# A fused two-model kernel on one core: the feed-forward's first projection with the weight tile as the stationary operand

## The reference

```python
def rms_norm(x, g):
    y = x * rsqrt(mean(x * x, axis=-1) + 1e-6)      # one factor per row, "rs" below
    return y * g
def swiglu(x, w1, w2):                               # w1: 1024 x 5632, w2: 2816 x 1024
    gu = x @ w1
    g, u = gu[..., :2816], gu[..., 2816:]
    return (silu(g) * u) @ w2
x = x + 0.5 * swiglu(rms_norm(x, norm), w1, w2)      # factor 1.0 in place of 0.5 in the last two
```

## Time and profile before

| what | us |
|---|---|
| median of 3 runs (2015.02 to 2015.93) | 2015.71 |
| the profiled execution's own time | 2013.65 |
| its span in the profile | 2011.8 |
| PE busy | 1993.3 (99%) |
| DVE busy | 1222.3 (61%) |
| ACT busy | 1027.0 (51%) |
| POOL busy | 282.6 (14%) |

### The profile page before, as it was taken

One profiled execution on the slowest core, in us unless ns is written; L12 is line 12 of the kernel. 1 busy time (PEld: TensorE's weight loads), 2 busy tenths in 40 slices (PEclk: granted clock), 3 DMA queues, 4 the chain that ended last, 5 costly groups with the idle time before them and its releaser, 6 DMA issues.

```text
span 2011.8 us, 26376 instructions
## 1 busy us (share of the span) xinstructions
PE 1993.3 (99%) x9796; PEld 1647.4 (82%) x9796; DVE 1222.3 (61%) x1438; ACT 1027.0 (51%) x1318; POOL 282.6 (14%) x365
## 2 busy tenths in 40 slices
PE   8999999999999999999999999999999999999998
PEld 7888887788888888887788888888888888788886
DVE  5555799865546555798855556556565555545554
ACT  5444676754444444686654436454554445455443
POOL 1000469200000000468200002111100000000000
PEclk9999999999999999999999999999999999999999
DMA  7554454455554554554445544443435554415552
GB/s 268 200 187 175 173 204 160 176 188 188 188 188 186 184 188 183 181 196 165 178 176 197 186 183 168 148 148 144 147 126 209 188 188 168 176 66 200 187 187 94
DMA packets 54627, 354.16 MB, mean 176 GB/s; under 512 B 7696, under 2 KB 8336, under 8 KB 12816
## 3 DMA queue, kind: packets, MB, share of 16 engines
q1 hardware_dynamic: 53968, 352.51, 48.5%
q10 hardware_dynamic: 576, 0.53, 0.1%
HBM read 351.97 MB, written 1.05 MB: 175 GB/s over the span
## 4 chain that ended last, share of the span: by engine, by line
PE 89%; DVE 6%; ACT 2%; DVEq 1%; issue 1%; DMA 0%; SPq 0%; POOLq 0%; ACTq 0%; POOL 0%
PE psum L1953 63%; PE psum L2010 18%; DVE wlo L1104 3%; PE psum L2088 1%; PE psum L2025 1%; DVE psum L1331 1%; PE psum L2425 1%; PE psum L2446 1%; PE psum L1965 1%; PE psum L2432 1%; ACT whi L587 1%; DVEq L1323 1%; PE psum L2136 0%; DMA raw<-w_stream 0%; PE psum L2165 0%
## 5 line engine op out<-in xcount | busy, mean ns | idle before, releaser
L1104 DVE TENSOR_TENSOR wlo<-raw,whi 128x2048 fp32r<-128x2048 f32 x325 | 751.5, 2315 | 388.8 <-ACT whi L587 386.4
L1953 PE MATMUL psum<-whi,xTh 128*128 128x512 f32 (+1 forms) x1920 | 763.2, 398 | 5.1 <-DVE xTl L1121 3.9
L1953 PE MATMUL psum<-whi,xTl 128*128 128x512 f32 (+1 forms) x1920 | 745.0, 388 | 0.0
L1953 PE MATMUL psum<-wlo,xTh 128*128 128x512 f32 (+1 forms) x1920 | 744.6, 388 | 0.0
L587 ACT ACTIVATE whi<-raw 128x2048 fp32r<-128x2048 f32 x325 | 622.0, 1916 | 238.3 <-PE psum L2010 151.6
L1953 PEld LDWEIGHTS psum<-whi,xTh 128*128 128x128 f32 x1920 | 360.7, 188 | 81.8 <-issue 6.3
L1953 PEld LDWEIGHTS psum<-whi,xTl 128*128 128x128 f32 x1920 | 360.5, 188 | 75.6
L1953 PEld LDWEIGHTS psum<-wlo,xTh 128*128 128x128 f32 x1920 | 361.2, 188 | 68.0
L2010 PE MATMUL psum<-whi,braT 128*128 128x512 f32 x1056 | 337.8, 390 | 0.0
L2010 PEld LDWEIGHTS psum<-whi,braT 128*128 128x128 f32 x1056 | 198.2, 188 | 41.2
L2010 PE MATMUL psum<-wlo,braT 128*128 128x512 f32 x528 | 205.5, 389 | 0.0
(11 more groups left out here) (258 smaller groups left out, 1460.5 us busy)
## 6 DMA issues: line engine op xcount, KB each, us to landing
raw<-w_stream SPq DMA_DIRECT2D x326, 1024.0 KB, 4.8
bias<-chunks SPq DMA_DIRECT2D x18, 256.0 KB, 5.0
x<-x_in SPq DMA_DIRECT2D x2, 512.0 KB, 5.3
raw<-w_stream SPq DMA_DIRECT2D x4, 256.0 KB, 7.6
arena<-gate_w SPq DMA_DIRECT2D x2, 512.0 KB, 5.0
arena<-fins SPq DMA_DIRECT2D x2, 512.0 KB, 5.5
con<-consts SPq DMA_DIRECT2D x1, 720.0 KB, 11.1
out<-x ACTq DMA_DIRECT2D x2, 256.0 KB, 2.3
```

The lines of the kernel that those rows point to most:

```text
L1104: TT(wlo[:, r], raw[:, r], whi[:, r].bitcast(F32), ALU.subtract).then_inc(lo_done, 1)
L1953: ins = pe.matmul(dst(rb), s(kt)[:, rows], w[:, r, at_:at_ + cols], start=start and n == 0 and k == 0, stop=stop and n == len(kts) - 1 and ...
```

## The change

The first projection is turned round. A 128x128 tile of the weights is stationary and x moves; what comes out has the columns of h on the partitions, so h needs no transposes (`turn_h` is gone). `xTh` and `xTl` become two halves of one tensor `xT`, and one move of 512 columns takes both parts of x past `whi`. The third product, `wlo` against the high part of x, is a move of 256 columns. For each of the 8 contraction tiles and 4 groups of 128 weight columns there is one wide (512) and one narrow (256) move: 32 wide and 32 narrow in a unit, where 48 wide ones stood. Moves of one width are put in groups of 4 or 8. The high-times-high and high-times-low sums lie in two halves of a bank, and must be added. `up` uses four banks: 0 to 3 in unit 0, 4 to 7 in all others.

After it, ACT copies the low half of the gate out of PSUM (`copied`), DVE adds the high half and multiplies by rs, ACT takes silu, ACT and DVE copy and add the up half, DVE multiplies, ACT makes h's high part and DVE its low part, all on tiles of 128 x 512. As rs now runs along the free dimension, it is needed as a row on every partition: ACT's DMA queue stores rs to memory (`rs_dram`) and loads it back broadcast into `rs_row`, once in each feed-forward. The up half is left without rs, and the residual multiplies by `rs_out` (rs times 0.5 or 1.0, a new POOL instruction ahead of `r_done`).

The diff, cut to its core:

```diff
-        xTh, xTl = sb("xTh", [P, KT, S], F32R), sb("xTl", [P, KT, S], F32R)
+        xT = sb("xT", [P, KT, 2, S], F32R)
+        xTh, xTl = xT[:, :, 0], xT[:, :, 1]
...
+        def up_bank(j):
+            return 0 if isinstance(j, int) and j == 0 else 4
...   ACT, ffn
                 split(b, 0)
+                act.wait_ge(r_done, b.norm + 1)
+                act.dma_start(rs_dram.rearrange("(p r) -> p r", r=RB), rs).then_inc(rs_stored, 16)
                 split(b, 1)
+                act.wait_ge(rs_stored, b.ffn * 16 + 16)
+                act.dma_start(rs_row[:], rs_dram.partition_broadcast(P)).then_inc(rs_row_in, 16)
+                def copied(j):
+                    n = b.ffn * UNITS + j
+                    act.wait_ge(gate_in, n + 1)
+                    if not (isinstance(j, int) and j == 0):
+                        act.wait_ge(up_out, n)
+                    act.activation(f_lo[:, 0:2], up_half(j, 0, 1), ACT.Copy).then_inc(low_copied, 1)
+                    unit_products(act, b, j)
+                    act.activation(f_lo[:, 2:4], up_half(j, 1, 1), ACT.Copy).then_inc(low_copied, 1)
                 def silu(j):
-                    unit_products(act, b, j)
-                    for rb in range(RB):
-                        act.activation(f_sg[:, rb], gate_up(b, j)[:, rb, 0:256], ACT.Silu, scale=rs[:, rb:rb + 1]).then_inc(silu_done, 1)
+                    act.wait_ge(gate_scaled, b.ffn * UNITS + j + 1)
+                    act.activation(f_g, f_g, ACT.Silu).then_inc(silu_done, 1)
...
                 unit(UNITS - 1, ahead=2)
+                h_hi(UNITS - 1)
                 if not b.final:
                     split(b, 3 * UNITS - 2)
-                h_hi(UNITS - 1)
...   DVE, ffn
-                def h_rows(j):
-                    for rb in range(RB):
-                        dve.wait_ge(silu_done, b.ffn * (2 * UNITS) + j * 2 + (rb + 1))
-                        ins = STT(f_h[:, rb], gate_up(b, j)[:, rb, 256:512], rs[:, rb:rb + 1], f_sg[:, rb], ALU.mult, ALU.mult)
-                    ins.then_inc(h_row, 1)
+                def sums(j):
+                    n = b.ffn * UNITS + j
+                    if isinstance(j, int) and j == 0:
+                        dve.wait_ge(rs_row_in, b.ffn * 16 + 16)
+                    dve.wait_ge(low_copied, 2 * n + 1)
+                    TT(f_g, up_half(j, 0, 0), f_lo[:, 0:2], ALU.add)
+                    dve.drain()
+                    by_row = f_g.rearrange("p t (r c) -> p t r c", r=RB)
+                    by = rs_row[:].rearrange("p (c r) -> p r c", r=RB).unsqueeze(1).to_broadcast([P, 2, RB, P])
+                    TT(by_row, by_row, by, ALU.mult).then_inc(gate_scaled, 1)
+                    dve.wait_ge(low_copied, 2 * n + 2)
+                    TT(f_u, up_half(j, 1, 0), f_lo[:, 2:4], ALU.add).then_inc(up_out, 1)
+                def h(j):
+                    dve.drain()
+                    dve.wait_ge(silu_done, b.ffn * UNITS + j + 1)
+                    TT(f_u, f_u, f_g, ALU.mult).then_inc(h_done, 1)
...   PE, ffn
+                    if not (start or half or (isinstance(j, int) and j == 1)):
+                        pe.wait_ge(up_out, b.ffn * UNITS + j)
...
+                    if half and not start:
+                        order = narrow(every, (0, 1)) + wide(every, (0, 1)) + narrow(every, (2, 3)) + wide(every, (2, 3))
+                    elif half:
+                        order = [x for k in every for x in narrow([k], every) + wide([k], every)]
+                    elif start and b.early:
+                        order = [x for ms in ((0, 1), (2, 3)) for x in wide([0], ms) + narrow(range(2), ms) + wide([1], ms)]
+                        order += wide([2], every) + narrow((2, 3), every) + wide([3], every)
+                    else:
+                        order = wide([0], every) + narrow((0, 1), every) + wide((1, 2), every) + narrow((2, 3), every) + wide([3], every)
...
+                        if start and b.early and (kt, m) == (0, 2):
+                            pe.wait_ge(x_done, b.x + 4)
+                        dst, at_ = psum[:, up_bank(j) + m], k * W + m * P
+                        if is_wide:
+                            ins = pe.matmul(dst, whi[:, r, at_:at_ + P], xT[:, kt].rearrange("p a s -> p (a s)"), start=kt == 0, stop=kt == KT - 1)
+                            if (kt, m) == (KT - 1, 1):
+                                ins.then_inc(gate_in, 1)
+                        else:
+                            pe.matmul(dst[:, 0:S], wlo[:, r, at_:at_ + P], xT[:, kt, 0], start=False, stop=False)
-                def turn_h(j):
-                    for rb in range(RB):
-                        pe.wait_ge(tdve, b.tdve + j * 2 + (3 + rb))
-                        for t in range(2):
-                            ins = pe.transpose(psum[:, 6 + rb, t * P:(t + 1) * P], f_h[:, rb, t * P:(t + 1) * P], ident)
-                        ins.then_inc(turned, 1)
...   POOL, rms
+                TS(rs_out, rs, b.ffn_scale, None, ALU.mult)
                 TS(rs8, rs, HD ** -0.5, None, ALU.mult).then_inc(r_done, 1)
```

More of the change, by code:

```diff
@@ L49 @@
 NORM_TURNS = [(f"norm{b}", "split") for b in range(4)]
[L50 removed]
+FFN_TURNS = NORM_TURNS
 MIX_TURNS = (NORM_TURNS + [("glu0", "act"), ("glu1", "act"), ("val0", "dve"), ("val1", "dve"), ("lx0", "act"), ("lx1", "act"),
@@ L392, in unit_products, with up_half @@
             eng.wait_ge(slot_used, b.slot + (2 if isinstance(j, int) and j == 0 else j * 3 + 1))
[L394 to L398, removed]
+        def up_bank(j):
+            return 0 if isinstance(j, int) and j == 0 else 4
+        def up_half(j, part, low):
+            first = up_bank(j) + 2 * part
+            return psum[:, first:first + 2, low * S:(low + 1) * S]
         def h_of(b, j, part):
@@ L584, in split @@
                 act.wait_ge(loaded[r], (third(b, i + 2) + thirds - (ring(b, i + 2) == 0)) * 16 + 16)
-                if not (i == 0 and isinstance(more, int)):
+                if not (i == 0 and isinstance(more, int) and more == 0):
                     act.wait_ge(slot_used, b.slot + more + i)
@@ L1283, in ffn @@
                     dve.wait_ge(fin_in, 32)
-                    residual(0, b.ffn_scale, ready, ((0, 0), (1, 0)))
+                    residual(0, rs_out, ready, ((0, 0), (1, 0)))
                     last_rows(0, 0)
@@ L1296, in ffn @@
                 next_norm(b)
-                residual(0, b.ffn_scale, ready, ((1, 0), (1, 1)))
+                residual(0, rs_out, ready, ((1, 0), (1, 1)))
                 if b.next and b.next.by_residue:
@@ L1994, in ffn, with up @@
                     busy(5)
-                def up(i, half, ready=never, more=0, j=1):
-                    ins = use(b, i, [(4 * half + k, k * W) for k in range(4)], W, xh, xl, ready, lambda rb: gate_up(b, j)[:, rb],
-                              half == 0, half == 1, more=more)
+                def up(i, half, j, ready=never, more=0):
+                    r, start = ring(b, i), isinstance(j, int) and j == 0
+                    first = start and half == 0 and not b.early
+                    if not (start or half or (isinstance(j, int) and j == 1)):
+                        pe.wait_ge(up_out, b.ffn * UNITS + j)
+                    if not first:
+                        pe.wait_ge(lo_done, b.slot + more + (i + 1))
+                    wide = lambda ks, ms: [(k, m, True) for k in ks for m in ms]
+                    narrow = lambda ks, ms: [(k, m, False) for k in ks for m in ms]
+                    every = range(4)
+                    if half and not start:
[7 more added lines that the diff above has]
+                        order = wide([0], every) + narrow((0, 1), every) + wide((1, 2), every) + narrow((2, 3), every) + wide([3], every)
+                    seen = set()
+                    for k, m, is_wide in order:
+                        kt = 4 * half + k
+                        if k not in seen:
+                            seen.add(k)
+                            if first and k < 3:
+                                pe.wait_ge(piece_lo, k + 1)
+                            elif first:
+                                pe.wait_ge(lo_done, 1)
+                            ready(kt)
+                        if start and b.early and (kt, m) == (0, 2):
[7 more added lines that the diff above has]
+                            pe.matmul(dst[:, 0:S], wlo[:, r, at_:at_ + P], xT[:, kt, 0], start=False, stop=False)
```

66 lines of the change are left out of this document (29 added, 37 removed).

## The result

The changed kernel took 2025.38 us (median of 5 runs, 2023.35 to 2027.64), the kernel before 2015.49 beside it (5 runs, 2013.92 to 2015.93): a ratio of 1.0051, interval 1.0037 to 1.0066. The forecast was 2003.3 and a range of 1994 to 2022. The profiled execution took 2025.21 us, 11.6 more than that of before (2013.65).

The account below looks back on a forecast made before the run. PE, busy 99% of the span, was taken to bound the kernel. Terms -30.6 + 15.0 + 2.5 + 0.7 = -12.4 us took 2013.65 to 2001.3, and 2.1 for the median gave 2003.3 us; range 1994 to 2022.

Parts of the forecast that it names:

- Turns of h and narrow moves: PE in all 66 units: removing the transposes of h saves 30.6 us, narrow moves at 0.1205 us add 15.0.
- Changes of width: Eight borders a unit between 256- and 512-column moves on PE: taken as 0, bounds 0 to 43.8 us in all.
- The rival with the highest time: Width changes cost up to 0.083 us at each of eight borders a unit: 2047 us; chance 0.11.
- The last unit: End of five feed-forwards: the residual ends later, transposes still start 8.67 us after `up`, giving a turn back: +2.5 us.
- The first unit: Start of a feed-forward: `up` takes banks 2 and 3 early and waits 0.15 us for the residual: +0.7 us.
- The row factor by DMA: Unit 0 of each feed-forward, starting at T0: rs stored and loaded back by T0 + 15.2: 0, bounds 0 to 12 us.
- The store's moment: Unit 0 of a feed-forward: the store of rs leaves ACT's queue at T0 + 9.2.
- the chain behind the row factor: Unit 0: from rs in its row through gate, silu and slot 4's parts to h's low part, 7.15 us.
- the latest harmless moment: Unit 0: rs in its row by T0 + 15.9 delays nothing, as `down` wants h at T0 + 23.1.
- The step from the profiled execution to the median: Whole kernel: the median of the runs lies 2.1 us above the profiled execution, taking 2001.3 to 2003.3.
- PE standing over 1 us before `down` of unit 0: Sign in the changed profile, at unit 0 of a feed-forward, that would show the prediction wrong.
- The rival for it: rs comes late: PE stands before `down` of unit 0 up to 2.0 us six times, 2009 to 2015; chance 0.14.

Follow-up runs that it names:

- e4: Changed kernel with wide and narrow moves alternating one by one in all units but the first, some 62 width changes a unit, not 8: 2033.41 us, ratio 1.009.
- e7: Kernel of e5 with the narrow moves of a slot together, four changes of width a unit in place of eight: 2003.76 us, ratio 0.995.
- e5: Kernel of e1 with DVE's low part of the next phase's first weight slot moved behind the residual's first two quarters: 2006.63 us, ratio 0.9959.
- e1: Changed kernel with the row factor spread by a PE product of ones and identity times rs, without DMA: 2007.64 us, ratio 0.9964.
- e2: Changed kernel without the store and its wait; the load goes early and reads another input, so values are not rs: 2005.89 us, ratio 0.9958.
- e6: Changed kernel with store and wait kept, the load reading another input at the same moment, values not rs: 2015.43 us, one execution.
- e3: Changed kernel with ten unneeded 512-column PE moves before the first `down` of each feed-forward: 2021.0 us, ratio 1.0029.

## Why the prediction was wrong

**Turns of h and narrow moves: right.** A narrow move costs 0.120 to 0.121 us by the units of the changed kernel, e4 and e7 taken together; the forecast took 0.1205. The unit was forecast at 16.56 and is 16.60.

**Changes of width: right within a little.** Taken as 0, they are 0.003 to 0.007 each (e4, e7). The rival with the highest time, at up to 0.083, was priced from the slow start behind four transposes; that row changes more than the width.

**The last unit: right in mechanism.** 0.3 of the 0.5 us of the turn is given back; the transposes come at 8.48 and not 8.67 us after the last `up`, and e5 shows the low part ahead of the residual as the cause.

**The first unit: right in kind, small.** The transposes of the entry to those of the next block are 6.47 to 6.81 us apart where they were 6.33 to 6.37, +1.6 us in all where 0.7 stood.

**The row factor by DMA: the step that failed.** The store's moment, the chain behind the row factor, and the latest harmless moment were right. What failed is the load's duration: I bounded it by 2.3 to 5.0 us from transfers of other kinds elsewhere in the kernel, took 3.7, and it took 6.4 (the store took 2.9 to 3.0 where I took 2.3), so the row factor came at T0 + 18.5 and not at T0 + 15.2, beyond the upper bound of 17.9 too. The text even noted the slot that DVE releases at T0 + 11.5, and left it as a reason for the upper end. The term was put at 0, with 12 us as the most; it cost 20: 12.9 for standing, and 7.2 for the slower unit behind it (6.4 of it the clock), which was nowhere in the working. e1 takes both away and lands at 2007.64, and e2 at 2005.89, beside a forecast of 2003.3; 2.5 of e1's 4.3 us are its product.

**The step from the profiled execution to the median.** The forecast added 2.1 us for it. That is about the size of one clock fall at the start (e7), and of the executions of a kernel some have it and some don't.

**The bets.** The prediction said that PE standing over 1 us before `down` of unit 0 would make it wrong, and it stands 1.84 to 2.69 us there. The rival for it stood at 2009 to 2015 with a chance of 0.14; even as a rival it had neither the load's size nor the clock. Its bound for the standing, 2.0 us a feed-forward, was nearly met (12.9 / 6 = 2.15).

Open: what makes the clock fall behind one wait and not behind another; what the 1.3 us between the feed-forwards are; why the load stands behind nearly a whole slot, and what the store ahead of it adds; whether the way by DMA could be kept, with the slot held back until rs is in its row.

## What to carry to other kernels

A DMA on the path is priced in the stretch where it will fly: look what else is due at that moment, since a load that takes 2.9 us alone took 6.4 when issued half a microsecond behind a slot of weights. When a wait is put in front of a full TensorE, price the wait and what the granted clock does behind it. A value per row that has to be spread over the partitions can go by a product with ones in 2.6 us for 0.4 us of PE, where store and load took 9.4.

## What the runs showed of the hardware

- A broadcast load of 1 KB into 128 partitions (128 KB) landed in 2.9 us with the DMA engines idle (e2) and in 6.0 to 6.4 with weights under way (e6, the changed kernel). Its first packet began after 0.97 us in the first case and after 3.9 to 4.9 behind a slot issued 0.2 to 0.6 us before it. Its store of 1 KB took 2.9.
- Behind PE's standing before the first `down` the granted clock fell to its lower level in four of six feed-forwards of the changed kernel, and how long PE had stood does not sort them. It fell behind 2.36, 1.92, 2.04 and 2.02 us, and not behind 1.84 and 2.69. Two of the six in PE's timeline, the second and the last feed-forward:

```profile
453.04 0.50 PE L2079 MATMUL psum<-whi,braT 128*128 128x512 f32 x1 [1.92 <-DVE braT L1282]
...
1855.53 0.50 PE L2079 MATMUL psum<-whi,braT 128*128 128x512 f32 x1 [2.69 <-DVE braT L1282]
```

and the same two in the chain:

```profile
453.04 7.36 PE psum L2079 x24
...
1855.53 5.73 PE psum L2079 x24
```

  The shorter wait has the slow 24 moves behind it. In e6 none of six (up to 1.8 us) had. In e4 five of six had (1.92 to 2.13 us; 0.48 had not). At the start of the program waits of 2.15, 2.25, 2.26 and 2.27 us (e3, e4, e1, e5) were followed by a fall, 2.24, 2.24, 2.27, 2.28 and 2.60 (e6, e7, e2, the kernel before, the changed kernel) were not. What decides stays open. A fall costs 1.6 to 1.7 us.
- Moves of 512, 384, 256 and 160 columns behind loads of 128: 0.227, 0.174, 0.120, 0.112 us; a change of width adds 0.003 to 0.007.
